# The modulation of layer 0: from multiply-and-sum rows on VectorE to column-tiled matmuls on TensorE

## What is computed

```
mods = (silu(cond) @ w_ada + b_ada)        # 1024 -> 6 * 1024, for two conditions (latent, context)
shift1, scale1, gate1, shift2, scale2, gate2 = split(mods, 6)
h = rms_norm(x) * (1 + scale1) + shift1
u = h @ w_in                               # pooling, q/k/v of 8 attention heads, gated linear attention
x = x + gate1 * concat(pool_mixer, neighbourhood_attention, gated_linear_attention) @ w_out
h2 = rms_norm(x) * (1 + scale2) + shift2
x = x + gate2 * swiglu(h2)
```

## Time and profile before

| | |
|---|---|
| median of three runs | 1785.93 us (1784.6 to 1788.76) |
| the profiled execution | 1783.07 us |
| its span, first to last instruction | 1781.3 us |
| PE (TensorE matmul) busy | 1637.7 us, 92% |
| PEld (TensorE weight load) busy | 1573.6 us, 88% |
| DVE (VectorE) busy | 1097.7 us, 62% |
| ACT (ScalarE) busy | 539.2 us, 30% |
| POOL (GpSimd) busy | 623.2 us, 35% |
| the chain that ended last | PE 78%, DVE 15% |

### The profile page before, as it was taken

How to read it: one execution, slowest core, us unless ns; L and a number is a source line. 1 busy time by engine, 2 the same in 40 slices (tenths; PEclk the granted TensorE clock), 3 DMA queues, 4 the chain that set the end, 5 groups by cost and what they waited for, 6 DMA issues and landing times.

```text
span 1781.3 us, 27593 instructions
## 1 busy us (share of the span) xinstructions
PE 1637.7 (92%) x11384; PEld 1573.6 (88%) x11384; DVE 1097.7 (62%) x1886; ACT 539.2 (30%) x890; POOL 623.2 (35%) x295
## 2 busy tenths in 40 slices
PE   3798888889999999999988799898999999999997
PEld 3687777779999999999988788787999999999997
DVE  7887687866788588757737856667644313431341
ACT  2232244343222122212333224544332212221232
POOL 3135211116343334343462441121533333333335
PEclk9897899999999999999998789999999999999999
DMA  9410133312343444344231102221222222222212
GB/s 362 149 61 15 59 112 115 114 36 95 107 154 130 166 142 148 137 142 155 82 103 57 40 24 66 66 70 47 72 72 72 71 75 80 71 72 75 80 60 95
DMA packets 54508, 171.44 MB, mean 96 GB/s; under 512 B 6832, under 2 KB 15728, under 8 KB 54000
## 3 DMA queue, kind: packets, MB, share of 16 engines
q1 hardware_dynamic: 54384, 169.68, 28.7%
HBM read 165.86 MB, written 3.80 MB: 95 GB/s over the span
## 4 chain that ended last, share of the span: by engine, by line
PE 78%; DVE 15%; issue 2%; DMA 2%; ACT 2%; POOL 0%; SPq 0%; DVEq 0%; ACTq 0%
PE acc L1305 55%; PE acc L1288 13%; PE acc L1325 2%; PE banks_OX L1477 2%; PE banks_OX L1515 1%; DVE banks_OX L786 1%; DVE weights L1138 1%; DMA w_ada<-in_w_gate 1%; DVE means L836 1%; DVE kk L812 1%; PE bank_S L1460 1%; PE bank_S L1414 1%; PE banks_OX L1444 1%; DVE mod_w L812 1%; DVE means L834 1%
## 5 line engine op out<-in xcount | busy, mean ns | idle before, releaser
L513 POOL TENSOR_TENSOR w_lo<-w_raw,w_hi 128x1024 fp32r<-128x1024 f32 (+1 forms) x196 | 506.2, 2584 | 1046.2 <-ACT w_hi L591 1046.1
L591 ACT ACTIVATE w_hi<-w_raw 128x1024 fp32r<-128x1024 f32 (+1 forms) x196 | 205.4, 1049 | 659.0 <-PE acc L1305 458.8
L1305 PE MATMUL acc<-h_hi,w_hi 128*128 128x320 f32 (+1 forms) x1440 | 331.4, 311 | 0.5 <-DVE means L1238 0.5
L1305 PE MATMUL acc<-h_lo,w_hi 128*128 128x320 f32 (+1 forms) x1440 | 331.4, 311 | 0.0
L1305 PEld LDWEIGHTS acc<-h_hi,w_hi 128*128 128x128 f32 x1440 | 243.2, 189 | 2.5 <-issue 0.9
L1305 PEld LDWEIGHTS acc<-h_lo,w_hi 128*128 128x128 f32 x1440 | 242.8, 189 | 0.0
L1305 PE MATMUL acc<-h_hi,w_lo 128*128 128x320 f32 (+1 forms) x1440 | 231.1, 313 | 0.0
L1305 PEld LDWEIGHTS acc<-h_hi,w_lo 128*128 128x128 f32 x1440 | 220.1, 190 | 0.0
L1198 DVE SCALAR_TENSOR_TENSOR x<-acc,mods,x 128x320 f32<-128x320 f32 (+2 forms) x192 | 72.6, 434 | 213.7 <-PE acc L1305 201.5
L1305 PE MATMUL acc<-y_lo,w_hi 128*128 128x320 f32 x808 | 184.0, 309 | 0.0
L1305 PE MATMUL acc<-y_hi,w_hi 128*128 128x320 f32 x808 | 183.9, 309 | 0.0
(11 more groups left out here) (248 smaller groups left out, 2194.1 us busy)
## 6 DMA issues: line engine op xcount, KB each, us to landing
w_raw<-in_w SPq DMA_DIRECT2D x176, 512.0 KB, 3.6
mod_w<-in_w_ada SPq DMA_DIRECT2D x72, 512.0 KB, 3.6
bias<-in_bias SPq DMA_DIRECT2D x48, 192.0 KB, 2.6
w_ada<-in_w_ada SPq DMA_DIRECT2D x16, 512.0 KB, 10.0
w_raw<-in_w SPq DMA_DIRECT2D x16, 384.0 KB, 3.1
w_ada<-in_w_gate SPq DMA_DIRECT2D x8, 512.0 KB, 8.7
x<-in_x SPq DMA_DIRECT2D x1, 2560.0 KB, 10.0
out_x<-x SPq DMA_DIRECT2D x1, 2560.0 KB, 7.5
```

Source lines behind the costliest of these rows:

```text
L513: pool.tensor_tensor(w_lo[p][:, 0:n], raw[p][:, 0:n], w_hi[p][:, 0:n].bitcast(F32), ALU.subtract).then_inc(lo_made[p], 1)
L591: act.activation(w_hi[p][:, 0:n], raw[p][:, 0:n], ACT.Copy).then_inc(hi_made[p], 1)
L1305: mm = pe.matmul(acc[p][:, half, 0:rows.shape[1]], w[:, k * P:(k + 1) * P], rows, start=w is w_hi[p] and k == 0 and m is hi, stop=w is w_l ...
```

## The change

All of shift1, scale1, gate1, shift2 and scale2 of layer 0 is made by TensorE with the roles turned round: the condition is stationary (two columns, filled up to 32 with zeros), and the weights move. Four such matmuls stand in the four column groups of the array, each with another eighth of the 1024 inputs, and two rounds of four make one group (`rows_of`). The result has outputs along the row, as four partial sums on 4 times 32 partitions; another engine copies it to SBUF, and a matmul of each 128 outputs with a constant `pick` sums the four parts and turns the outputs onto the partitions (`turn`).

At the start there are four groups of 512 outputs (shift1, scale1); VectorE copies them out. The loads are reordered: `x` first, then the groups, the five parameters that only later stages need behind the first weight tiles. The refinement of the root now stands ahead of the last group's copy. Gate1, shift2 and scale2 become twelve units of 256 outputs, at the steps 10, 13, ... 43, as fills of bank `X` that ScalarE copies out, and three turns at the steps 21, 33 and 45, which VectorE adds to the bias. A unit's weights are 1 MB, in two slots that lie where `cond_rows` and `mod_w` come later. `cond_rows` is loaded and its SiLU taken only at the end of the mixers. The rows made in the feed-forward part stay on VectorE.

```diff
+def mod_unit_at(step):
+    return [r for r in range(MOD_UNITS) if step == 10 + 3 * r]
+def mod_turn_at(step):
+    return [i for i in range(MOD_UNITS // UNITS_TURNED) if step == 10 + 3 * (UNITS_TURNED * i + UNITS_TURNED - 1) + 2]
...
+    if l == 0:
+        out += [("unit", r) for r in mod_unit_at(step)] + [("turn", i) for i in mod_turn_at(step)]
...
-MOD_ROWS = [(0, SHIFT2 + n) for n in range(2 * KT)]
-FIRST_MOD_STEP = 12
+MOD_ROWS = []
...
             sp.dma_start(cond[:], a["cond"]).then_inc(cond_in, 16)
-            sp.dma_start(cond_rows[:], a["cond_rows"]).then_inc(rows_in, 16)
...
             sp.dma_start(x[:], a["x"]).then_inc(x_in, 16)
+            load_first(0)
+            for m, t in (("pick", pick), ("mats", mats), ("b_ada", b_ada), ("small", small_all)):
                 sp.dma_start(t[:], a[m]).then_inc(par_in, 16)
+            for n in range(1, FIRST_GROUPS):
+                load_first(n)
+            def load_unit(r):
+                if r >= 2:
+                    sp.wait_ge(full["X"], after("X", ("unit", r - 2), 0))
+                sp.dma_start(unit_w[r % 2][:], a["w_unit"][r]).then_inc(unit_in[r % 2], 16)
...
                 for t in range(T_OUT):
+                    load(t)
+                    if l == 0 and t == T_K:
+                        for m, dst in (("rope", rope), ("causal", causal), ("heads4", heads4), ("edges", edges),
+                                       ("inv_w", inv_w)):
+                            sp.dma_start(dst[:], a[m]).then_inc(rest_in, 16)
+                    if l == 0 and t == T_PAIR:
+                        load_unit(0)
+                        load_unit(1)
                     if l == 0:
+                        for r in range(2, MOD_UNITS):
+                            if t == T_PAIR + 3 + r * 9 // 10:
+                                load_unit(r)
...
-            pool.wait_ge(par_in, 16 * NPAR)
+            pool.wait_ge(rest_in, 16 * NREST)
...
+                    for name in x_fills_at(g - 1, l):
+                        if name[0] == "unit":
...
+                            act.wait_ge(full["X"], after("X", name, l))
+                            act.activation(unit_rows[:, r % UNITS_TURNED * UNIT_WIDE:(r % UNITS_TURNED + 1) * UNIT_WIDE],
+                                           X[:, 0:UNIT_WIDE], ACT.Copy).then_inc(free["X"], 1)
...
                 act.preload_act_table(ACT.Silu)
+                if l == 0:
+                    act.wait_ge(rows_in, 16)
+                    act.activation(cond_rows[:], cond_rows[:], ACT.Silu).then_inc(rows_made, 1)
...
-            for n in range(NROWS):
-                dve.wait_ge(ada_in[n % ROW_SLOTS], 16 * (n // ROW_SLOTS + 1))
-                for s in range(2):
...
+            def copy_first(n):
+                dve.wait_ge(first_made, n + 1)
+                dve.tensor_copy(first_rows[n], first_banks[n]).then_inc(first_copied, 1)
+            for n in range(FIRST_GROUPS - 1):
+                copy_first(n)
...
+                if l == 0:
+                    finish_root("n1")
+                    copy_first(FIRST_GROUPS - 1)
+                    dve.wait_ge(first_turned, FIRST_GROUPS)
+                    link(dve.tensor_tensor(mods[:, 0:2 * KT, :], O[:, 0:4 * KT].rearrange("p (m s) -> p m s", s=2),
+                                           wide(b_ada[:, 0:2 * KT], 2), ALU.add))
...
+                        if name[0] == "turn":
+                            take("X", name)
+                            first = (GATE1, SCALE2, SHIFT2)[name[1]]
+                            dve.tensor_tensor(mods[:, first:first + KT, :], X[:, 0:2 * KT].rearrange("p (m s) -> p m s", s=2),
+                                              wide(b_ada[:, first:first + KT], 2), ALU.add).then_inc(free["X"], 1)
...
-                    if l == 0 and 0 <= g - FIRST_MOD_STEP < 4 * KT:
-                        mod_product(rows_done, (g - FIRST_MOD_STEP) % 2, unused)
-                        rows_done += (g - FIRST_MOD_STEP) % 2
...
-            for n in range(NMID - NROWS):
-                slot = ROW_SLOTS + n % COL_SLOTS
-                pe.wait_ge(ada_in[slot], (n // COL_SLOTS + 1) * 16)
+            def rows_of(dst, w, wide_):
                 for k in range(KT):
+                    c = k % 4
+                    mm = pe.matmul(dst[32 * c:32 * c + 32, 0:wide_], cond[:, k, :], w[:, k, :], start=k < 4, stop=k >= 4,
+                                   tile_position=(0, 32 * c))
+                return mm
+            def turn_first(n):
+                pe.wait_ge(first_copied, n + 1)
+                for i in range(4):
+                    m = 4 * n + i
+                    mm = pe.matmul(O[:, 2 * m:2 * m + 2], first_rows[n][:, i * P:(i + 1) * P], pick[:], start=True, stop=True)
+                mm.then_inc(first_turned, 1)
+            first_group(0)
             pe.wait_ge(par_in, 16 * NPAR)
+            for n in range(1, FIRST_GROUPS - 1):
+                first_group(n)
+                turn_first(n - 1)
...
                 norm(0)
+                if l == 0:
+                    first_group(FIRST_GROUPS - 1)
+                    turn_first(FIRST_GROUPS - 2)
+                    turn_first(FIRST_GROUPS - 1)
                 both_tiles(T_LR, h_is_made)
...
+                        if kind == "unit":
+                            pe.wait_ge(unit_in[i % 2], 16 * (i // 2 + 1))
+                            claim("X", name)
+                            rows_of(X, unit_w[i % 2], UNIT_WIDE).then_inc(full["X"], 1)
+                        if kind == "turn":
+                            pe.wait_ge(free["X"], 1 + after("X", ("unit", UNITS_TURNED * (i + 1) - 1), l))
+                            claim("X", name)
+                            for m in range(KT):
+                                mm = pe.matmul(X[:, 2 * m:2 * m + 2], unit_rows[:, m * P:(m + 1) * P], pick[:], start=True, stop=True)
+                            mm.then_inc(full["X"], 1)
```

More of the change, by code:

```diff
@@ L55 @@
 WN = NT // 2
-NPAR = 9
+NPAR, NREST = 4, 5
 LRW = 32
@@ L115, in gla_outs_at, with x_fills_at @@
     return [j for j in range(NP) if step == 5 + j]
-EARLY_FILLS, LATE_FILLS = ("vtr",), ("qsum", "ksum", "gsum", "pool")
-def x_fills_at(step):
+EARLY_FILLS, LATE_FILLS = ("vtr",), ("qsum", "ksum", "gsum", "pool", "unit", "turn")
+def mod_unit_at(step):
+    return [r for r in range(MOD_UNITS) if step == 10 + 3 * r]
+def mod_turn_at(step):
+    return [i for i in range(MOD_UNITS // UNITS_TURNED) if step == 10 + 3 * (UNITS_TURNED * i + UNITS_TURNED - 1) + 2]
+def x_fills_at(step, l):
     out = [("go", j) for j in gla_outs_at(step)]
@@ L139, with fills_of_layers @@
     "O": ["zb", "rq", "va1", "kdb", "uba"] + [("go", j) for j in range(NP)],
-    "X": ["zb", "rq", "va1", "ubb"] + [f for g in range(STEPS) for f in x_fills_at(g)],
-}
+    "X": ["zb", "rq", "va1", "ubb"] + [f for g in range(STEPS) for f in x_fills_at(g, l)],
+} for l in range(DEPTH)]
 ROOTS = ["n1", ("q", 0), ("k", 0), ("g", 0), ("q", 1), ("k", 1), ("g", 1), ("q", 2), ("k", 2), ("q", 3), ("k", 3), "n2"]
 NR = len(ROOTS)
+def fills_of_layers(bank, l):
+    return sum(len(FILLS[i][bank]) for i in range(l))
 def before(bank, name, l):
-    return l * len(FILLS[bank]) + FILLS[bank].index(name)
+    return fills_of_layers(bank, l) + FILLS[l][bank].index(name)
 def after(bank, name, l):
@@ L239, in build @@
         vT = sb("vT", [P, T])
+        with ExitStack() as first:
+            unit_w = [sb(f"unit_w{p}", [P, KT, UNIT_WIDE], F32, first) for p in range(2)]
         cond_rows = sb("cond_rows", [P, 2, D])
@@ L252, in build @@
         with ExitStack() as first:
-            ada = [sb(f"w_ada{s}", [P, KT * P], F32, first) for s in range(ROW_SLOTS + COL_SLOTS)]
+            first_w = [sb(f"first_w{n}", [P, KT, FIRST_WIDE], F32, first) for n in range(FIRST_GROUPS)]
         with ExitStack() as first:
@@ L324, in build @@
         pooled = (root, means1)
-        unused = kk[:, 1].rearrange("p d c i n -> p (d c i n)")
+        unit_rows = kk[:, 1].rearrange("p d c i n -> p (d c i n)")
+        first_rows = (gla_o[:, 0, 0:FIRST_WIDE], gla_o[:, 1, 0:FIRST_WIDE], qn[:, 0, 0:FIRST_WIDE], qn[:, 1, 0:FIRST_WIDE])
+        first_banks = [acc[n // 2][:, n % 2, :] for n in range(FIRST_GROUPS)]
         scaled_rows = (tmp[:, 0, 0:T], tmp[:, 1, 0:T], padded[:, 0:T], means1)
@@ L395, in _, with load_first @@
-            for n in range(4):
-                load_row(n)
-            load_col(0)
-            load_col(1)
-            for n in range(4, ROW_SLOTS):
-                load_row(n)
-            load_col(2)
             sp.dma_start(x[:], a["x"]).then_inc(x_in, 16)
-            load_col(3)
-            for m, t in (("mats", mats), ("b_ada", b_ada), ("small", small_all), ("rope", rope),
-                         ("causal", causal), ("heads4", heads4), ("edges", edges), ("inv_w", inv_w),
-                         ("state", state_in)):
+            def load_first(n):
+                sp.dma_start(first_w[n][:], a["w_first"][n]).then_inc(first_in[n], 16)
```

(13 more changed lines are left out.)

116 lines of the change are left out of this document (50 added, 66 removed).

## The result

The changed kernel takes **1768.65 us** (median of 4 runs, 1767.35 to 1770.31) against 1786.94 for the kernel before beside it (1784.6 to 1788.76): ratio 0.9903, 95% interval 0.9891 to 0.9915. The forecast was 1769.9 us, with a range of 1756 to 1783; the kernel is faster by more than 0.2%. So the medians are 18.3 us apart. Six more runs of the same kernel in a later comparison gave 1772.22 us against 1786.00 (ratio 0.9915, 0.9899 to 0.9931), 13.8 apart. The profiled execution took 1769.7 us, 13.4 less than the profiled one of before, which lies 3.9 under its median.

The account below looks back on a forecast made before the run. VectorE's products were taken to bound the start, and TensorE nearly the mixers. Start -23.7 and layer 0's mixers +7.7 gave -16.0: profiled 1783.07 to 1767.1, with the median's 2.9 on top 1769.9 us, range 1756 to 1783.

Parts of the forecast that it names:

- The start: Up to TensorE's first tile product: 32 VectorE products go, first product at 48.5 us, 23.7 us less, bounds 20.4 and 28.
- warm chain: Start: TensorE at 2.4 GHz, the chain waits for group 2's load at 27.0 and ends at 46.0; at 1.2 GHz 51.8.
- The mixers: Layer 0, first tile product to output product: 341.3 us, 7.7 more than before, bounds nothing more and 21.3 more.
- values and transposes behind ScalarE's copy: Layer 0's mixers, five steps where values follow a unit: wait for a copy of about 0.38 us, 1.5 us in all.
- I put these 20.7 us on the path whole: Layer 0's mixers: TensorE's twelve units (13.9 us) and three turns (6.8) lengthen the stretch by their full time.
- turns: Layer 0's mixers: three on TensorE, each 16 x 0.13 + 0.2 us, 6.8 us in all.
- units behind means: Layer 0's mixers: six units wait until VectorE empties the mean, 6.0 us less 3.8 of present waits, 2.2 us.
- VectorE's sum after a turn is hidden behind turned probabilities: Layer 0's mixers, after each turn: VectorE's addition to the bias adds no wait.
- A: Layer 0's mixers: TensorE's present gaps take half of the 20.7 us, no new waits; 326.3 us, total 1754.9. Chance 0.14.
- B: Start and mixers: column tiles do not run at the same time, a unit takes 3.46 us; total 1814 us. Chance 0.05.
- C: Layer 0's mixers: bank `X` becomes the bound, fifteen fills wait 40 us instead of 4.7; total 1805 us. Chance 0.09.
- SyncE and tile 19: Layer 0's mixers: weight tile 19 queues behind loads of units 10 and 11; one wait of 1 us, bounds 0 and 4.

Follow-up runs that it names:

- the five in one: Changed kernel with the last five of each unit's eight matmuls all on the last column tile: 1782.79 us, ratio 0.9986 to the kernel before.

## Why the prediction was right, and where not

**The start, -25.6 for -23.7, within its bounds.** The chain was the one described: group 2's load, norm, root, last copy, last turn, scaling. I had put 46.0 for a warm chain and 51.8 for a cold one and taken 48.5 between; 46.59 is near the warm one, in part by luck. The two groups ahead of group 2 ran cold and that cost nothing, because group 2 waits for its load. But that load came 0.7 us later than forecast, and group 2 ran cold too, 3.33 us at a granted clock of 0.56 for the 1.92 of group 3. VectorE's refinement made up for it: 2.7 us (35.65 to 38.36), with GpSimd idle beside it, for the 4.05 that I took from the kernel before. From the norm to the last turn TensorE was warm. The squares ended at 24.5 us for the 28 forecast (11.63 us of GpSimd for 16.35, with VectorE nearly idle beside them), hidden by the same load.

**The mixers, +9.1 for +7.7.** The steps are 26.5 us above layer 1's, where the forecast's terms make 25.4. Right: units 13.7 us (forecast 13.9), values and transposes behind ScalarE's copy 1.3 (1.5); "I put these 20.7 us on the path whole" held, as the run without units shows. The Trainium skill's figure ("TensorE: Matmul & The Clock Gate", Part 3) gave an estimate of 1.09 us a unit ahead of its start and end; here it is too high, since a unit with both takes 1.07 us at full clock and two in a row take 1.93. Too high: turns, 5.5 us for 6.8. Too low: units behind means cost 6.5 less 2.2 given back, 4.3 for 2.2; I took all 3.8 us of present waits as given back.

**The step that failed** is "VectorE's sum after a turn is hidden behind turned probabilities". I asked who waits for the sum, and nobody does; I did not ask what stands behind it in VectorE's queue. In loop 22 that is a norm that sets a wait of TensorE: 3.49 us where the run without units waits 1.93. Moving the sum behind the norm takes 2.7 us off this wait and 2.5 off the steps. The two later waits of this kind are 2.9 us together for 4.0 without units, so the row as a whole grows by 0.5 only.

**What no term had.** The clock is one: from loop 9 on, these are the changed kernel and the run without units:

```profile
163.30:371.74 208.44, 187.60 (x1392) 158.09 (x1393) 112.60 (x314) 84.22 (x199) 28.85 (x12) 0.94 0.31 106
```

```profile
163.90:345.31 181.41, 164.63 (x1152) 145.52 (x1153) 116.80 (x311) 80.46 (x187) 28.61 (x12) 0.95 0.20 61
```

TensorE is busy 23.0 us longer, of which units and turns are 19.2; the other 3.8 lie in products that the run without units has too, here at a granted clock of 0.94 for 0.95. The other is what waits of values behind pooling gave in return, 4.1 us for 6.1. The account is then 19.2 of work, 4.1 of waits (4.3 + 1.3 + 0.5 - 2.0) and 3.8 of slower products, less 0.5 ahead of loop 9: 26.6 for the 26.5. That the total came out near the forecast is in part luck, since work and waits were forecast 2.1 too high and the 3.8 were not forecast at all. The same holds for the time: the medians' 18.3 and 13.8 lie on either side of the forecast's 16.

**The rivals.** A is out for the places that the change gave its units, and right about the gaps: the run with units in front of waits takes most of them up. Against A I had written that the longest wait, in pooling, lies behind the last unit; that was a matter of placement, and two units and a turn went there. B is out: a unit takes 1.07 us for its 3.46, and the five in one shows that the tiles work side by side. C is out: the named waits of units and values for units, turns and copies come to 8 us, far from 40, and a bank of their own gives 5.1 in the steps.

**SyncE and tile 19:** ScalarE waited once, 2.1 us, for that tile (forecast 1, bounds 0 and 4); none of TensorE's waits is put down to it. No run took this wait away alone, so what it costs was not tried.

## What to carry to other kernels

Work added to an engine that runs in order can be free where it stands in front of a wait that the engine has anyway, and writes where nobody else writes at that time: here the same twelve units and three turns cost 26.6 us between steps, and by the steps nothing with half of the units and the turns in front of waits. Look for what stands behind a small instruction that waits for another engine: a 0.17 us add held up a ready norm, and through it the busiest engine. And look at the clock behind a wait on TensorE: two waits of 3.5 us were followed by half-speed products that cost 4.4 us more, and both went with the waits; in another loop the half-speed products stayed when the wait went.
